# Sparse attention's exponentials cut by halves of the keys, sliding attention's row maximum cut by halves of the heads

## The chip, the core and the metric

The kernel runs on one NeuronCore of a Trainium2 chip. Five engines work from queues of their own, each strictly in the order in which the kernel lists its instructions, and are tied to one another by semaphores only: PE (TensorE, matrix products and transposes), DVE (VectorE), ACT (ScalarE, exponentials and copies), POOL (GpSimd) and SP (SyncE, which starts most DMA transfers). The metric is the device time of one execution in microseconds (us); lower is better.

## The reference

One transformer block for 2048 tokens of width 1024: a projection, three kinds of token mixing side by side, an output projection, a mixture of experts and a gated embedding. The change lies in two of the three mixers.

```python
def dsa_mixer(...):                      # sparse attention, 4 heads
    for each block of 128 queries:       # keys 0 .. end of the block
        sel = top_k(score, 256)
        logits = q @ k[sel] + bias
        probs = softmax(logits)          # exp(l - max) / sum
        out = probs @ v[sel]

def swa_mixer(...):                      # sliding attention, 8 heads, 256 keys a block
    m = maximum(max(logits), sink)
    e = exp(logits - m)
    probs = e / (sum(e) + exp(sink - m))
    out = probs @ v
```

## The kernel before

The selection of the 256 keys has become a mask by the time the function `mixers` starts. `mixers` runs three streams in one: sparse attention (a), sliding attention (w) and the gated linear mixer (g). Each is a list of items; each item has a due time, and all are merged into the one list `items`. Every engine walks through the same list and issues its own part of each item, so the order on each engine is fixed by that list.

**Sparse attention** works in 32 units u: 16 blocks of 128 queries, in the order `ORDER` (block 2, 6, 10, 14, 15, 13, 12, 11, 9, 8, 7, 5, 4, 3, 1, 0), times two pairs of heads. Block j has 128(j+1) keys, that is `steps_of(u)` = j//2+1 steps of 256 keys. The items of a unit:

- Q (u, ci): PE computes the logits of up to 512 keys for two heads into `psL` (L1468; `psL` has one buffer, shared with the item q). DVE adds the mask into `logits` (L1618), takes the maximum of each chunk (L1622, L1633), then of all chunks (L1636) and its negative (L1640).
- E (u, 0) and E (u, 1): ACT takes the exponential in place over all keys of head 0, then of head 1, with the row sum as a by-product into `den` (L1368).
- T (u, sp): PE transposes 256 keys of both heads into a bank of `psX` (L1479), ACT copies the bank to `PT` (L1378). The first T of a unit waits for both exponentials (L1474). `psX` has five banks, used in turn by all three streams.
- V (u, sp): PE multiplies `PT` with the values (L1490), two steps behind its T.
- P and O: ACT copies the result (L1385), PE turns it back (L1499), DVE takes the reciprocal of `den` (L1647) and multiplies (L1652).

For a unit of n steps before it, E (u+1, 0) stands behind step n-3 and E (u+1, 1) behind step n-2 of unit u, so between the two lie one T of unit u with its copy and whatever the other streams have there; with two steps or one, both stand together behind the first step.

**Sliding attention**, block n of 128 queries: q (n, 0) and q (n, 1) each compute half of the eight heads (two of each group of four) into `psL` (L1513); DVE adds the bias into `lg` (L1674). After the second, DVE takes the maximum over all eight heads (L1679), then three small steps (L1680 to L1682); ACT takes eight exponentials (L1390); t, v and o transpose (L1522), multiply (L1535) and turn back (L1543).

When `mixers` ends, SP waits for its last stores, and the next stage (`mix`) starts by loading `o_dram` (L1896).

Of the kernel before, what the change touches and what calls it, by code (L numbers as in the profile page):

```python
# [17 lines left out]
P = 128  # L18
# [992 lines left out]
def mixers(nc, outer, used, kA, small, loads, mask_dram, o_dram, y_dram, ident):  # L1011
# [3 lines left out]
    with ExitStack() as ctx:  # L1015
        def sb(name, shape, dt=F32):
            return ctx.enter_context(nc.sbuf_tensor("p2_" + name, shape, dt))
# [22 lines left out]
        parts = sb("parts", [P, 2, 2, NCH])  # L1040
        den = sb("den", [P, 2, AH])
        rden = sb("rden", [P, 2, AH])
# [40 lines left out]
        biased, top_done, neg_ready, exp_done = sem("biased"), sem("top_done"), sem("neg_ready"), sem("exp_done")  # L1083
        part_done = sem("part_done")
        pv_done, oT_done, rden_done = sem("pv_done"), sem("oT_done"), sem("rden_done")
# [15 lines left out]
        def steps_of(u):  # L1101
            return block_of(u) // 2 + 1


# [243 lines left out]
        def _(act):  # L1348
# [10 lines left out]
            for item in items:  # L1359
                kind = item[0]  # L1360
                if kind == "E":
# [4 lines left out]
                    if (i, h) == (0, 0) and at >= 2:  # L1366
                        act.wait_ge(rden_done, AP2 * (at - 1))
                    act.activation(logits[:, u % 2, h, 0:W], logits[:, u % 2, h, 0:W], ACT.Exp, bias=top[:, u % 4, 1, h:h + 1],  # L1368
                                   accum_out=den[:, at % 2, 2 * i + h:2 * i + h + 1]).then_inc(exp_done, 1)
                    if (i, h) == (1, 0) and at + 1 < NT:  # L1370
# [84 lines left out]
        def _(pe):  # L1455
            pe.wait_ge(both_set, 1)
            for item in items:
# [12 lines left out]
                elif kind == "T":  # L1470
                    u, sp = item[1], item[2]
                    j = block_of(u)
                    if sp == 0:
                        pe.wait_ge(exp_done, 2 * (u + 1))  # L1474
                    until_empty(pe, item)
# [119 lines left out]
        def _(dve):  # L1595
# [9 lines left out]
            for item in items:  # L1605
                kind = item[0]
                if kind == "Q":
# [16 lines left out]
                    else:  # L1624
# [5 lines left out]
                        if u >= 4:  # L1630
                            dve.wait_ge(exp_done, 2 * (u - 3))
                        if ci:
# [8 lines left out]
                elif kind == "O":  # L1641
                    u = item[1]
                    at, i = divmod(u, AP2)
                    dve.wait_ge(exp_done, 2 * (u + 1))
                    if u >= 4:
                        until_read(dve, ("O", u - 4))
                    dve.reciprocal(rden[:, at % 2, 2 * i:2 * i + 2], den[:, at % 2, 2 * i:2 * i + 2]).then_inc(rden_done, 1)  # L1647
                    dve.wait_ge(rden_done, u + 1)
# [6 lines left out]
                elif kind == "q":  # L1655
# [9 lines left out]
                    if n == 0:  # L1665
                        for a in (2 * part, 2 * part + 1):
                            heads = lambda t: t.rearrange("p (g a) k -> p g a k", g=SKV)[:, :, a, first:KEYS]
                            ins = dve.tensor_tensor(heads(lg[:, 0, :, :]), psL[:, :, (a % 2) * KEYS + first:(a % 2 + 1) * KEYS], heads(nearW[:, :, :]), ALU.add)
                            if a % 2 == 0:
                                dve.wait_ge(w_step, after_w(ins))  # L1670
                        ins.then_inc(l_done, 1)
                    else:
                        heads = lambda t: t.rearrange("p (g a) k -> p g a k", g=SKV)[:, :, 2 * part:2 * part + 2, :]
                        dve.tensor_tensor(heads(lg[:, n % 2, :, :]), psL[:, :, :].rearrange("p g (a k) -> p g a k", a=2), heads(nearW[:, :, :]), ALU.add).then_inc(l_done, 1)  # L1674
                    if part == 1:
                        dve.wait_ge(l_done, l_use[item] + 1)
                        if n >= 2:
                            until_read(dve, ("o", n - 2))
                        dve.wait_ge(w_step, after_w(dve.tensor_reduce(st[0], lg[:, n % 2, :, :], AX, ALU.max)))  # L1679
                        dve.wait_ge(w_step, after_w(dve.tensor_tensor(st[1], st[0], sink[:, :], ALU.max)))  # L1680
# [1389 lines left out]
```

## Time and profile before

| | us |
|---|---|
| median of 3 runs | 2882.42 (2882.03 to 2883.32) |
| the profiled execution | 2880.68 |
| its span in the profile | 2879.0 |
| busy in the span | PE 2604.5, DVE 1807.8, ACT 1271.5, POOL 923.4 |

The span is the time from the first to the last instruction in the profile; 1.7 us of the execution lie around it. `mixers` runs from about 845 to 1401 us of the span. Busy time of an engine says how much work it had; what ends a stretch is read from the waits, that is, from what each engine was waiting for when it stood still. The chain that ended last, as the page gives it, covers only the final stage, so it says nothing on this one.

### The profile page before, as it was taken

The page shows a single profiled execution, that of the slowest core. Times are in us where ns is not written, and L with a number is a line of the kernel's source. Part 1 is how long each engine was busy: PE and PEld are TensorE (multiplying, and loading weights), DVE is VectorE, ACT ScalarE, POOL GpSimd, SP SyncE. Part 2 cuts the span into 40 slices and gives each one's busy share as a digit, 9 for nine tenths or more (in the row PEclk, how much of TensorE's full clock was granted, in tenths as well). Part 3 has the DMA queues.
Part 4 walks back from the last instruction along what each step waited for, and adds up shares of the span by engine and source line. Part 5 has one row for each costly group of instructions (what it writes and reads, how often), then busy time and mean ns, then how long its engine had stood idle before and what let it go on. Part 6 is the DMA issues. An engine that isn't in the chain of part 4 may idle for free. (4 is left out here: it accounts for less than half of the span.)

```text
span 2879.0 us, 34808 instructions
## 1 busy us (share of the span) xinstructions
PE 2604.5 (90%) x10908; PEld 1646.4 (57%) x10909; DVE 1807.8 (63%) x2522; ACT 1271.5 (44%) x2289; POOL 923.4 (32%) x925
## 2 busy tenths in 40 slices
PE   6988779999987888878799969999999999998998
PEld 3634323345843444444588846666666676665787
DVE  2176999699976877776333377654464336643676
ACT  2277868958955665665322222222222222221322
POOL 2377877600011111121000024434434335332321
PEclk9999989999989999899799989999999999999999
DMA  5101130113151123212544377986586655974663
GB/s 149 61 31 45 31 61 30 48 56 94 41 183 60 45 68 93 85 53 68 185 147 146 122 292 270 350 321 226 214 333 226 214 203 196 361 275 154 201 218 132
DMA packets 221473, 438.07 MB, mean 152 GB/s; under 512 B 22888, under 2 KB 91048, under 8 KB 221224
## 3 DMA queue, kind: packets, MB, share of 16 engines
q1 hardware_dynamic: 199400, 357.78, 36.3%
q0 software_dynamic: 13312, 47.32, 5.2%
q10 hardware_dynamic: 8640, 31.46, 2.7%
q8 instruction: 62, 1.02, 0.1%
q14 instruction: 59, 0.48, 0.1%
HBM read 331.14 MB, written 105.38 MB: 152 GB/s over the span
## 5 line engine op out<-in xcount | busy, mean ns | idle before, releaser
L2468 DVE CAST p_high<-p_low 128x2048 fp32r<-128x2048 f32 x128 | 203.9, 1593 | 400.1 <-PE p_psG L2575 292.7
L698 PE MATMUL p_psP<-home,p_ring 128*128 128x512 f32 x832 | 366.3, 598 | 0.0
L2591 PE MATMUL p_psY<-p_wd,p_hT 128*128 x752 | 330.9, 593 | 2.2 <-ACT p_hT L2650 1.9
L2470 DVE TENSOR_TENSOR p_low<-p_low,p_high 128x2048 fp32r<-128x2048 f32 x128 | 319.0, 2492 | 4.4
L698 PEld LDWEIGHTS p_psP<-home,p_ring 128*128 128x128 f32 x832 | 157.3, 191 | 205.0 <-issue 204.9
L2591 PEld LDWEIGHTS p_psY<-p_wd,p_hT 128*128 128x128 f32 x752 | 139.3, 190 | 160.5 <-issue 160.4
L727 PE MATMUL p_psI<-p_kI,p_qI 64*128 64x512 f32 (+3 forms) x608 | 148.0, 595 | 62.9 <-ACT p_relu L589 62.8
L2511 POOL TENSOR_TENSOR p_xT_low<-p_xT,p_xT_high 128x512 fp32r<-128x512 f32 x94 | 186.0, 1997 | 3.4 <-ACT p_xT L2635 3.4
L2573 PE MATMUL p_psG<-p_high,p_xT_high 128*128 128x512 f32 x376 | 166.5, 443 | 15.8 <-DVE p_low L2470 8.2
L603 ACT ACTIVATE p_relu<-p_relu,p_small 128x512 f32<-128x512 f32 (+3 forms) x266 | 161.4, 662 | 0.0
L2517 POOL TENSOR_TENSOR p_hid<-p_act_g,p_act_u 128x512 f32<-128x512 f32 x47 | 62.4, 1327 | 308.1 <-ACT p_act_u L2645 295.2
L2573 PE MATMUL p_psU<-p_high,p_xT_high 128*128 128x512 f32 x376 | 154.3, 410 | 6.0 <-DVE p_low L2470 6.0
L2656 ACT ACTIVATE p_y<-p_psY 128x512 f32<-128x512 f32 x94 | 56.2, 598 | 220.3 <-PE p_psY L2591 220.3
L2574 PE MATMUL p_psG<-p_low,p_xT_high 128*128 x376 | 149.7, 398 | 0.0
L2575 PE MATMUL p_psG<-p_high,p_xT_low 128*128 128x512 f32 x376 | 149.7, 398 | 0.0
L589 ACT ACTIVATE p_relu<-p_psI 128x1024 f32<-128x1024 f32 (+3 forms) x152 | 136.4, 914 | 28.6 <-PE p_psI L727 10.4
L2574 PE MATMUL p_psU<-p_low,p_xT_high 128*128 x376 | 148.5, 395 | 0.0
L2575 PE MATMUL p_psU<-p_high,p_xT_low 128*128 128x512 f32 x376 | 148.4, 395 | 0.0
L2641 ACT ACTIVATE p_act_g<-p_psG 128x512 f32<-128x512 f32 x47 | 28.1, 598 | 260.7 <-PE p_psG L2575 260.7
L727 PEld LDWEIGHTS p_psI<-p_kI,p_qI 64*128 64x128 f32 x608 | 50.9, 191 | 152.1 <-ACT p_relu L589 109.9
L2645 ACT ACTIVATE p_act_u<-p_psU 128x512 f32<-128x512 f32 x47 | 28.1, 597 | 240.7 <-PE p_psU L2575 240.7
L1618 DVE SCALAR_TENSOR_TENSOR p_logits<-p_mask,p_psL 128x1024 f32<-128x1024 uint8 (+3 forms) x80 | 84.7, 1059 | 71.5 <-PE p_psL L1468 69.6
(421 smaller groups left out, 5847.4 us busy)
## 6 DMA issues: line engine op xcount, KB each, us to landing
p_low<-in_w_expert_gate_dram SPq DMA_DIRECT2D x32, 2048.0 KB, 13.4
p_low<-in_w_expert_up_dram SPq DMA_DIRECT2D x32, 2048.0 KB, 16.8
p_wd<-in_w_expert_down_dram SPq DMA_DIRECT2D x32, 2048.0 KB, 10.7
y_dram<-p_y ACTq DMA_DIRECT2D x47, 512.0 KB, 8.2
p_xt<-in_x_dram SPq DMA_DIRECT2D x32, 512.0 KB, 4.6
y_dram<-p_clear SPq DMA_DIRECT2D x32, 512.0 KB, 4.5
proj_f<-p_stage SPq DMA_DIRECT2D x52, 256.0 KB, 2.4
p_ot<-o_dram SPq DMA_DIRECT2D x16, 512.0 KB, 4.3
```

What stands on the lines that cost most here:

```text
L589: act.activation(relu[:, n % NRELU, :, 0:c1 - c0], psI[:, n % NI, :, 0:c1 - c0], ACT.Relu).then_inc(relu_done, 1)
L603: act.activation(dst, src, ACT.Copy, scale=small[:, j, h:h + 1]).then_inc(weighed, 1)
L698: mm = pe.matmul(psP[0:n, i % 2, :], w, aT[:, k, c * CH:(c + 1) * CH], start=k == 0, stop=k == KD - 1)
L727: mm = pe.matmul(psI[:, n % NI, half, 0:c1 - c0], qI[r, b % 2, i, :], kI[r, c0:c1], start=True, stop=True)
L1618: dve.scalar_tensor_tensor(out=dst[:, :, c0:c1], in0=hidden, scalar=NEG, in1=psL[:, :, 0:c1 - c0], op0=ALU.mult, op1=ALU.add).then_inc(l_d ...
L2468: dve.tensor_copy(high[:, m, k, :], low[:, par, m, k, :].bitcast(F32)).then_inc(high_done, 1)
L2470: dve.tensor_tensor(low[:, par, m, k, :], low[:, par, m, k, :].bitcast(F32), high[:, m, k, :].bitcast(F32), ALU.subtract).then_inc(w_split, 1)
L2511: pool.tensor_tensor(xT_low[:, k, :], xT[:, k, :], xT_high[:, k, :].bitcast(F32), ALU.subtract).then_inc(xT_split, 1)
L2573: pe.matmul(ps[:, :], xT_high[:, k, :], high[:, m, k, :], start=k == 0, stop=False)
L2574: pe.matmul(ps[:, :], xT_high[:, k, :], left, start=False, stop=False)
L2575: mm = pe.matmul(ps[:, :], xT_low[:, k, :], high[:, m, k, :], start=False, stop=k == KD - 1)
L2591: mm = pe.matmul(psY[:, c, :], hT[:, k, :], wd[:, bass.ds(at, 1), k, c * CH:(c + 1) * CH].rearrange("p a f -> p (a f)"), start=k == 0, sto ...
```

## The change

`halves(u)` cuts the n steps of a unit in two: the first (n+1)//2 steps and the rest; a unit of one step (blocks 0 and 1) stays whole. The item E (u, h) now means "half h of the keys, both heads": two exponentials of half the width where there was one of the full width, each with a sum of its own, for which `den` has another dimension. The first T of a unit waits for the first half only, the T that begins the second half for the second. In item O, DVE adds the two sums into `rden`, waits for that, and takes the reciprocal. In sliding attention, each of q (n, 0) and q (n, 1) takes the maximum of its own four heads, right after adding the bias.

```diff
+        def halves(u):
+            n = steps_of(u)
+            return (0, (n + 1) // 2, n) if n > 1 else (0, n)
+
+        def exps_before(u):
+            return sum(2 * (len(halves(v)) - 1) for v in range(u))
...
-                    act.activation(logits[:, u % 2, h, 0:W], logits[:, u % 2, h, 0:W], ACT.Exp, bias=top[:, u % 4, 1, h:h + 1],
-                                   accum_out=den[:, at % 2, 2 * i + h:2 * i + h + 1]).then_inc(exp_done, 1)
+                    ends = [min(2 * P * sp, W) for sp in halves(u)]
+                    for k, head in [(0, h)] if len(ends) == 2 else [(h, 0), (h, 1)]:
+                        keys = slice(ends[k], ends[k + 1])
+                        act.activation(logits[:, u % 2, head, keys], logits[:, u % 2, head, keys], ACT.Exp, bias=top[:, u % 4, 1, head:head + 1],
+                                       accum_out=den[:, at % 2, k, 2 * i + head:2 * i + head + 1]).then_inc(exp_done, 1)
...
-                    if sp == 0:
-                        pe.wait_ge(exp_done, 2 * (u + 1))
+                    if sp in halves(u):
+                        pe.wait_ge(exp_done, exps_before(u) + 2 * (halves(u).index(sp) + 1))
...
-                    dve.reciprocal(rden[:, at % 2, 2 * i:2 * i + 2], den[:, at % 2, 2 * i:2 * i + 2]).then_inc(rden_done, 1)
+                    mine = slice(2 * i, 2 * i + 2)
+                    if len(halves(u)) == 2:
+                        total = den[:, at % 2, 0, mine]
+                    else:
+                        total = rden[:, at % 2, mine]
+                        dve.tensor_tensor(total, den[:, at % 2, 0, mine], den[:, at % 2, 1, mine], ALU.add).then_inc(summed, 1)
+                        dve.wait_ge(summed, sum(len(halves(v)) == 3 for v in range(u + 1)))
+                    dve.reciprocal(rden[:, at % 2, mine], total).then_inc(rden_done, 1)
...
+                    dve.wait_ge(l_done, l_use[item] + 1)
+                    if part == 0 and n >= 2:
+                        until_read(dve, ("o", n - 2))
+                    mine = lambda t: t.rearrange("p (g a) k -> p g a k", g=SKV)[:, :, 2 * part:2 * part + 2, :]
+                    reduced = after_w(dve.tensor_reduce(st[0].rearrange("p (g a) -> p g a", g=SKV)[:, :, 2 * part:2 * part + 2], mine(lg[:, n % 2, :, :]), AX, ALU.max))
                     if part == 1:
-                        dve.wait_ge(l_done, l_use[item] + 1)
-                        if n >= 2:
-                            until_read(dve, ("o", n - 2))
-                        dve.wait_ge(w_step, after_w(dve.tensor_reduce(st[0], lg[:, n % 2, :, :], AX, ALU.max)))
+                        dve.wait_ge(w_step, reduced)
```

## Rows read from the trace of the kernel before

**Rows 1.** Page, part 1: busy time of each engine over the whole span.
```profile
PE 2604.5 (90%) x10908; PEld 1646.4 (57%) x10909; DVE 1807.8 (63%) x2522; ACT 1271.5 (44%) x2289; POOL 923.4 (32%) x925
```
**Rows 2.** Windows: stretch, length, busy (count) PE PEld DVE ACT POOL, PEclk, DMA share, GB/s.
```profile
845.00:1400.00 555.00, 451.21 (x2556) 242.81 (x2556) 386.07 (x582) 331.83 (x773) 83.00 (x111) 0.91 0.22 70
1176.00:1190.00 14.00, 7.75 (x28) 4.35 (x28) 5.75 (x7) 9.91 (x13) 10.29 (x8) 0.56 0.20 69
```
**Rows 3.** Waits in 845 to 1400: who waited for whom, us, times, longest us.
```profile
PE p_psL L1468 <- DVE p_logits L1618: 28.3, 20, 2.3
PE p_psX L1479 <- ACT p_logits L1368: 24.8, 11, 6.0
PE p_psL L1513 <- DVE p_logits L1618: 11.3, 14, 2.2
PE p_psL L1468 <- DVE p_lg L1674: 8.1, 8, 1.8
...
PE p_psX L1543 <- ACT p_oTW L1407: 5.7, 3, 2.1
...
ACT p_logits L1368 <- DVE p_top L1640: 46.1, 19, 5.5
```
**Rows 4.** Timeline of PE, 855 to 1395: each first T that waited (start, us).
```profile
861.64 1.11 PE L1479 MATMUL p_psX<-ident,p_logits 128*128 128x128 f32 x4 [4.08 <-ACT p_logits L1368]
892.75 0.66 PE L1479 MATMUL p_psX<-ident,p_logits 128*128 128x128 f32 x4 [1.30 <-ACT p_logits L1368]
934.69 0.66 PE L1479 MATMUL p_psX<-ident,p_logits 128*128 128x128 f32 x4 [1.28 <-ACT p_logits L1368]
1038.82 0.66 PE L1479 MATMUL p_psX<-ident,p_logits 128*128 128x128 f32 x4 [2.02 <-ACT p_logits L1368]
1111.39 0.66 PE L1479 MATMUL p_psX<-ident,p_logits 128*128 128x128 f32 x4 [1.22 <-ACT p_logits L1368]
1136.90 0.66 PE L1479 MATMUL p_psX<-ident,p_logits 128*128 128x128 f32 x4 [0.50 <-ACT p_logits L1368]
1181.78 1.11 PE L1479 MATMUL p_psX<-ident,p_logits 128*128 128x128 f32 x4 [6.01 <-ACT p_logits L1368]
1238.71 0.66 PE L1479 MATMUL p_psX<-ident,p_logits 128*128 128x128 f32 x4 [0.75 <-ACT p_logits L1368]
1365.71 1.12 PE L1479 MATMUL p_psX<-ident,p_logits 128*128 128x128 f32 x4 [4.31 <-ACT p_logits L1368]
```
**Rows 5.** Timeline, 1385 to 1432: the first transfer and matmul of the next stage.
```profile
1403.71 0.32 SPq L1896 DMA_DIRECT2D p_ot<-o_dram  x1
...
1407.76 1.97 PE L1948 MATMUL p_psT<-ident,p_ot 128*128 128x128 f32 x8 [7.62 <-DMA p_ot<-o_dram]
```
**Rows 6.** Groups by form, 845 to 1400: count, busy us, mean ns of one, idle before.
```profile
L1390 ACT ACTIVATE p_lg<-p_lg,p_stats 128x256 f32<-128x256 f32 x128 | 63.4, 499 | 8.2 <-DVE p_stats L1682 8.2
L1368 ACT ACTIVATE p_logits<-p_logits,p_top 128x2048 f32<-128x2048 f32 x4 | 8.0, 1992 | 0.0
```
**Rows 7.** Timeline, 1168 to 1190: all engines around the longest wait.
```profile
1173.34 1.58 ACT L1368 ACTIVATE p_logits<-p_logits,p_top 128x1536 f32<-128x1536 f32 x1 [1.95 <-DVE p_top L1640]
...
1178.16 0.59 ACT L1378 ACTIVATE p_PT<-p_psX 128x512 f32<-128x512 f32 x1
...
1180.06 1.57 ACT L1368 ACTIVATE p_logits<-p_logits,p_top 128x1536 f32<-128x1536 f32 x1
...
1184.00 0.58 ACT L1378 ACTIVATE p_PT<-p_psX 128x512 f32<-128x512 f32 x1
...
1185.05 1.22 DVE L1618 SCALAR_TENSOR_TENSOR p_logits<-p_mask,p_psL 128x1024 f32<-128x1024 uint8 x1 [7.10 <-PE p_psL L1468]
```
**Rows 8.** Groups by form of DVE, 845 to 1400: maxima and a small step.
```profile
L1622 DVE TENSOR_REDUCE p_parts<-p_logits 128x2 f32<-128x1024 f32 x42 | 51.3, 1221 | 1.4
L1679 DVE TENSOR_REDUCE p_stats<-p_lg 128x8 f32<-128x2048 f32 x16 | 36.6, 2286 | 0.5
...
L1687 DVE TENSOR_TENSOR p_stats<-p_stats 128x8 f32<-128x8 f32 x16 | 2.5, 156 | 0.0
```

More of the change, by code:

```diff
@@ L1040, in mixers @@
         parts = sb("parts", [P, 2, 2, NCH])
-        den = sb("den", [P, 2, AH])
+        den = sb("den", [P, 2, 2, AH])
         rden = sb("rden", [P, 2, AH])
@@ L1083, in mixers @@
         biased, top_done, neg_ready, exp_done = sem("biased"), sem("top_done"), sem("neg_ready"), sem("exp_done")
-        part_done = sem("part_done")
+        part_done, summed = sem("part_done"), sem("summed")
         pv_done, oT_done, rden_done = sem("pv_done"), sem("oT_done"), sem("rden_done")
@@ L1630, in _ @@
                         if u >= 4:
-                            dve.wait_ge(exp_done, 2 * (u - 3))
+                            dve.wait_ge(exp_done, exps_before(u - 3))
                         if ci:
@@ L1643, in _ @@
                     at, i = divmod(u, AP2)
-                    dve.wait_ge(exp_done, 2 * (u + 1))
+                    dve.wait_ge(exp_done, exps_before(u + 1))
                     if u >= 4:
                         until_read(dve, ("O", u - 4))
-                    dve.reciprocal(rden[:, at % 2, 2 * i:2 * i + 2], den[:, at % 2, 2 * i:2 * i + 2]).then_inc(rden_done, 1)
+                    mine = slice(2 * i, 2 * i + 2)
[6 more added lines that the diff above has]
+                    dve.reciprocal(rden[:, at % 2, mine], total).then_inc(rden_done, 1)
                     dve.wait_ge(rden_done, u + 1)
```

## The prediction, written before the change was run

> **What bounds the kernel now.** I read the page first: PE is busy for 90% of the span, no other engine for more than 63% [rows 1]. The change touches only `mixers`, so the second view is the windows of that stretch, 845 to 1400. PE is busy for 451 of 555 us, DVE for 386, ACT for 332, and the granted clock is 0.91 [rows 2]. PE is the fullest engine here, but about 104 us of it are idle; what the change can win is in these, in the work that runs at half the clock, and nowhere else. The third view is the table of waits. PE's largest are for DVE to free `psL` (28.3, 11.3 and 8.1 us) and, second in the list, 24.8 us in 11 times for the exponentials of L1368 [rows 3]. The fourth is PE's timeline, which gives each of the 11: nine have their row, and the other two, of 1.73 and 1.60 us, are the rest of the 24.8 and belong to block 0, whose units of one step the change leaves whole [rows 3, 4]. What follows the stage isn't loaded ahead: the next stage's first transfer starts at 1403.7 and its first matmul waits for it [rows 5]. So time won in `mixers` moves all that follows, and nothing later hides it.
>
> **Part 1: the first T waits for half of the exponentials.** One exponential takes 499 ns for 256 keys and 1992 ns for 2048 [rows 6], that is (1992-499)/1792 = 0.833 ns a key and 286 ns that don't depend on the width. A pair of halves costs what one full one did, plus 286 ns. So E (u, 0) ends 0.29 us later than now, and the first T may start right behind it instead of behind E (u, 1).
>
> What each wait is worth, by the rows of PE [rows 4]. Seven belong to units whose predecessor has three steps or more, so that a T, its copy and other streams' work stand between the two E: 892.75 (1.30), 934.69 (1.28), 1038.82 (2.02), 1111.39 (1.22), 1136.90 (0.50), 1181.78 (6.01) and 1238.71 (0.75). In each, the first exponential's end plus 0.29 lies ahead of PE's last instruction before the wait, so the whole wait goes: 13.1 us. The two at 861.64 (4.08) and 1365.71 (4.31) have both E side by side right behind the maximum, for 384 and 512 keys; the wait is for the maximum, and only the second pair of short exponentials drops out: 0.5 and 0.7 us (by the formula, two of 384 keys take 2 x 606 ns and two of 256 take 2 x 499, which is 0.2; 512 keys likewise 0.4; a short copy of some 0.3 us that lies between the two E no longer stands ahead of T). Sum 14.3 us.
>
> Does the wait only move? The items behind a T are Q of the next unit and V of a step two back. For the 6.01 us I followed it through [rows 7]. The first E starts at 1173.34 and ends at 1174.9; two copies and a function-table change of another stream come next, then a copy at 1178.16, the second E at 1180.06, another table change and Silu, and a copy at 1184.00. PE could start T at 1175.8 and Q after it, do V when the copy of 1178.16 is there (1179.0 with the 0.29), then q, t and T, and would stand still at the V that needs the copy of 1184.00: with 2 x 0.29 added that is 1185.2. Now PE comes to this V at about 1190.0. So this wait gives 4.8 instead of 6.0, and the rest turns into a wait behind the copy. In the others the copies come with 0.6 us or more in hand. DVE speaks for a real gain: behind this T it stood 7.10 us waiting for Q's matmul [rows 7], so it wasn't the one that held PE. Part 1 gives 14.3 - 1.2 = **-13.1 us**.
>
> **Part 2: ACT pays for it.** 28 units of more than one step take two exponentials more each: 56 x 0.286 = 16.0 us. ACT has 555 - 332 = 223 us idle here [rows 2]; the cover is its waiting for PE and 46.1 us for the maximum [rows 3]. Bounds: at the low end nothing; at the high end all 16.0. What PE waits for of ACT's other work is small, the largest line 5.7 us [rows 3], all such lines together some 19 us by my addition, a fifth to a sixth of PE's idle time. I take that share of 16.0: **+3 us**. Behind each lengthened E on ACT are the copies of T, and PE's V waits for those.
>
> One rule of the Trainium skill speaks against this: "VectorE: DVE Perf Modes", section on the TRN2 errata, says that ScalarE and VectorE pay a fixed latency once per instruction that reads SBUF, and advises tiles of 512 elements or more. The rows agree on the price, 286 ns at any width; blocks below 8 get halves of under 512 keys, and by the rule their 12 units (24 extra exponentials, 6.9 us of ACT) were better left whole.
>
> **Part 3: the sum of the two denominators on DVE.** 28 additions, each a small step with the wait for its result. Nearest row: 156 ns for 128x8 [rows 8]; with the hand-over about 0.2 us: 5.6 us. They stand in item O, ahead of the reciprocal; queued behind are the multiplication into `ostA`, which frees a bank, and the next mask addition, which frees `psL`. Bounds 0 and 5.6.
>
> **Part 4: the sliding maximum in two.** One reduction of 2286 ns becomes two of about 1221 (same element count as L1622) [rows 8]: 0.16 us more each, 16 times, 2.5 us. But it also moves. The one in q (n, 1) is 1.07 us shorter, and DVE had its next work ready in 13 of 16 cases, so 13.9 us come off where DVE is late. The new one in q (n, 0) adds 1.22 us; in 7 of 15 cases DVE stood idle for 0.75 us or more right there, waiting for PE, and hides it, in 8 it delays what is behind: 9.8 us. Net -4.1. Parts 3 and 4 together: 5.6 - 4.1 = +1.5 us of DVE's hurried time. PE's waits for DVE are about half of its idle time [rows 3], but each such microsecond reaches PE only where `psL` or a bank is short; I take a third: **+0.5 us**. Bounds -3 and +8 (all of 5.6 + 2.5). The waits that move with it ask for things that DVE itself did long before and cost nothing. No DMA is moved, and POOL's instructions stay; its waits for earlier work of the linear mixer only shift along.
>
> **Clock.** In 1176 to 1190 the granted clock is 0.56 (nearly all at the lower level, 1.2 GHz), with PE busy for 7.75 of 14 us [rows 2], and the four transposes at 1181.78 take 1.11 us instead of 0.66 [rows 4]. Before this stretch PE had stood still for 6 us. Without it, up to 3.9 us (half of 7.75) would come back, but PE will still stand still for some 4.5 us in the same place. I take nothing, and keep it as a rival.
>
> **Sum.** -13.1 + 3 + 0.5 = -9.6, rounded -9.5 us. The profiled execution took 2880.7, so it would take 2871.2; the median of the runs is 1.7 above it, so the forecast is 2882.4 - 9.5 = **2872.9 us**.
>
> **Rivals.**
> (a) The wait moves. Once PE has run ahead by a T and a Q, it stands at the V behind ACT's copies or at one of the five banks, since ACT is a queue in fixed order and none of its copies comes earlier. For: I found it for the longest wait, 1.2 of 6.0. Against: behind the others the copies are there. If this took two thirds of part 1, -13.1 becomes -4.4, and with the costs -1: 2881.4 us.
> (b) Slower: ACT becomes the bound. The place is the copies queued behind the four exponentials of a unit; the price is 286 ns an exponential, 16.0 us in all, and 8.1 us of DVE's small steps beside it. It decides once more than half of the 24.1 us is on PE's path: at all of it, -13.1 + 24.1 = +11: 2893.4 us. Against it: ACT is idle for 40% of the stage.
> (c) The clock comes back too. Three of the stretches behind a wait ran their T at half speed, 1.11, 1.11 and 1.12 us [rows 4]. If each gives 3 us on top: -9.5 - 9 = -18.5: 2863.9 us. The Trainium skill, "TensorE: Matmul & The Clock Gate", section "Why this matters for your kernels", says that idle gaps between bursts of matmuls throw the clock back, which is this rival; the rows agree for 1181.78, and no row shows that shorter gaps keep it up.
> (d) The change doesn't do what it says for part 1, since a unit's second half is waited for as well. The T that begins the second half comes two to four steps later, behind an E that has long been issued, so I give it nothing but what (a) has.
>
> **How the numbers follow.** Chances: forecast 0.50 (from -6 to -14), (a) 0.27 (from +2 to -6), (c) 0.13 (from -14 to -22), (b) 0.10 (from +2 to +14). A measurement of this kernel can tell some 0.2%, 5.8 us, from no change. Faster by more than that: the forecast's cases, (c), and none of (a): 0.62. Slower by more: half of (b) and a little more, 0.07. Same: the remaining 0.31. The range: down to -20, since (c) reaches there, and up to +3, which holds (a) and the beginning of (b): 2862.4 to 2885.4, with about 0.1 left out on either side in all.
>
> **What would show it.** Right: in the table of waits, PE's 24.8 us for the exponentials fall to about 11 (3.6 + 3.6 + 3.3 for the maxima and block 0 remain), no wait of 6 us is left, ACT's busy time grows by some 16 us plus the read-outs of the sums, DVE's by some 8, and the stage ends 8 to 11 us earlier. If the waits fall and the stage doesn't end earlier, look for PE's waits for `PT` (L1378 before L1490) or for the copies of the other streams: (a). If ACT's idle time for PE is gone, (b). If the granted clock of the stage rises above 0.93, (c). The prediction is wrong altogether if the time changes outside 845 to 1400.

## The result: 0.5% faster, and the profile after

The changed kernel takes 2869.8 us (median of 6 runs, 2864.2 to 2872.0) where the one before takes 2882.2. The ratio is 0.9947, with a 95% interval of 0.9933 to 0.9960, that is 15.3 us less (11.5 to 19.3). The medians alone differ by 12.4. The runs below were made in three later rounds, each with runs of the kernel before beside it, so kernels are compared by their ratios: an effect in us is its ratio less one, times 2882; where two such effects are subtracted, each brings an uncertainty of 2 to 5 us.

The profiled execution took 2864.2 us, the shortest of the six, with a span of 2862.4. Page, part 1, of the kernel after (compare [rows 1]):

```profile
PE 2597.6 (91%) x10908; PEld 1643.8 (57%) x10909; DVE 1810.6 (63%) x2566; ACT 1284.8 (45%) x2401; POOL 923.7 (32%) x925
```

Where the time went is seen at the stage's end: the next stage's first transfer, 1403.71 before [rows 5], is now at 1388.45, and its first matmul waits for it as it did. So 15.3 of the 16.6 us between the spans lie inside `mixers`, and all that follows moved along. Timeline of after (start, us):

```profile
1388.45 0.32 SPq L1916 DMA_DIRECT2D p_ot<-o_dram  x1
...
1392.14 1.97 PE L1968 MATMUL p_psT<-ident,p_ot 128*128 128x128 f32 x8 [7.27 <-DMA p_ot<-o_dram]
```

The windows from the first unit's negative maximum (L1640 before, L1651 after) to that transfer, in both kernels (columns as in [rows 2]); first before, then after:

```profile
849.96:1403.71 553.75, 448.11 (x2543) 241.02 (x2541) 383.58 (x579) 330.97 (x771) 78.62 (x101) 0.91 0.22 69
```
```profile
850.56:1388.45 537.89, 441.42 (x2543) 238.34 (x2541) 386.53 (x623) 344.00 (x883) 79.33 (x101) 0.93 0.23 71
```

PE ran the same 2543 matmuls. Its idle time fell from 105.6 to 96.5 us, which gives 9.2 of the 15.9 us between these windows; the other 6.7 are the same matmuls taking 441.4 instead of 448.1 us, at a granted clock of 0.93 instead of 0.91.

PE's waits in 845 to 1388 of after (compare [rows 3]; L1379 is now the exponential, L1490 the transpose T, L1479 the matmul of Q, L1629 the mask addition, L1692 the sliding bias, L1501 V, L1396 and L1389 ACT's copies):

```profile
PE p_psL L1479 <- DVE p_logits L1629: 27.3, 23, 2.5
PE p_psL L1524 <- DVE p_logits L1629: 10.8, 14, 2.2
PE p_psX L1490 <- ACT p_logits L1379: 10.4, 4, 3.6
PE p_psL L1479 <- DVE p_lg L1692: 8.8, 9, 1.9
PE p_psX L1510 <- ACT p_oT L1396: 8.7, 8, 2.4
PE p_psX L1554 <- ACT p_oTW L1418: 6.6, 3, 2.6
...
PE p_psX L1546 <- ACT p_PTW L1412: 6.0, 4, 2.3
PE p_psX L1490 <- ACT p_PT L1389: 3.4, 3, 2.8
```

The 24.8 us in 11 times for the exponentials became 10.4 in 4, as forecast: what is left are the two units that wait for their maximum and block 0. But the waits for ACT's copies grew. The timeline of after around what was the longest wait [rows 7] shows both:

```profile
1166.93 0.60 PE L1490 MATMUL p_psX<-ident,p_logits 128*128 128x128 f32 x4
...
1167.46 1.13 PE L1479 MATMUL p_psL<-p_kA,near 64*128 64x512 f32 x4
...
1169.77 0.59 ACT L1389 ACTIVATE p_PT<-p_psX 128x512 f32<-128x512 f32 x1
...
1170.41 0.65 PE L1501 MATMUL p_psO<-p_PT,p_small 128*64 128x256 f32 x4 [1.82 <-ACT p_PT L1389]
...
1175.89 0.58 ACT L1389 ACTIVATE p_PT<-p_psX 128x512 f32<-128x512 f32 x1
...
1176.52 0.65 PE L1501 MATMUL p_psO<-p_PT,p_small 128*64 128x256 f32 x4
```

T runs at 1166.9 without a wait, before the second pair of exponentials, Q follows it, V waits 1.82 us for a copy, and the next V stands at 1176.5 right behind its copy of 1175.9, in the order in which the prediction walked it through. The maximum of the next unit comes 13.3 us earlier than before (1184.43 against 1197.74) where that of this unit came 8.7 earlier: 4.6 us, against the forecast 4.8. But the forecast was one of waiting alone. Windows from this unit's maximum to the next one's, before and after:

```profile
1173.14:1197.74 24.60, 18.11 (x92) 9.74 (x92) 15.83 (x21) 18.17 (x28) 10.29 (x8) 0.72 0.21 72
```
```profile
1164.46:1184.43 19.97, 15.81 (x88) 9.08 (x88) 18.23 (x23) 18.41 (x32) 10.32 (x8) 0.85 0.27 88
```

PE's idle time fell by 2.3 us (6.5 to 4.2). The other 2.3 is PE's busy time, at a granted clock of 0.85 instead of 0.72 and with four matmuls fewer between the two marks. (Up to the maximum of unit 18, where both kernels have 259 matmuls, it is 3.0 us of idle time and 2.7 of busy time.) That the two add up to nearly the 4.8 is a coincidence.

What the added work costs its engine, from the groups by form of after (compare [rows 6] and [rows 8]):

```profile
L1697 DVE TENSOR_REDUCE p_stats<-p_lg 128x4 f32<-128x1024 f32 x32 | 39.0, 1220 | 1.1
...
L1663 DVE TENSOR_TENSOR p_rden<-p_den 128x2 f32<-128x2 f32 x28 | 5.3, 191 | 0.0
```

Each of these is as the prediction had it (1221 and some 200 ns), and the exponentials' own time grew from 76.7 to 92.1 us, for a forecast of 16.0 more. ACT is busy for 13.0 us more and DVE for 3.0, where some 8 were forecast: the added reductions and sums are there (2.4 and 5.3 us), but other work of DVE became shorter, above all one pair of updates of `p_state` in the linear mixer. At 1062.24 of the kernel before the pair took 4.32 us while POOL ran two additions of 128x1024, and 1.13 us in the kernel after, where it ran ahead of them. No wait of PE is put down to that pair; DVE stood idle for 1.23 us behind it. Most of this looked like a forecast come true. The experiments say otherwise: the total was right, its parts weren't.

### The profile page after: what moved, and what is told of

It reads as the page before. It is cut to its first block and busy times, and to the rows that moved or that the text cites. A ratio compares the mean times of both kernels' runs of the same rounds, so it can differ in the third digit from the quotient of the medians.

```text
span 2862.4 us, 34991 instructions
## 1 busy us (share of the span) xinstructions
PE 2597.6 (91%) x10908; PEld 1643.8 (57%) x10909; DVE 1810.6 (63%) x2566; ACT 1284.8 (45%) x2401; POOL 923.7 (32%) x925
## 5 line engine op out<-in xcount | busy, mean ns | idle before, releaser
L589 ACT ACTIVATE p_relu<-p_psI 128x1024 f32<-128x1024 f32 (+3 forms) x152 | 136.5, 914 | 28.5 <-PE p_psI L727 10.4
L1479 PE MATMUL p_psL<-p_kA,near 64*128 64x512 f32 (+3 forms) x320 | 84.5, 603 | 42.1 <-DVE p_logits L1629 27.3
```

Source lines behind the costliest of these rows:

```text
L589: act.activation(relu[:, n % NRELU, :, 0:c1 - c0], psI[:, n % NI, :, 0:c1 - c0], ACT.Relu).then_inc(relu_done, 1)
L1479: mm = pe.matmul(psL[:, h, 0:c1 - c0], qA[r, at % 2, i, :], kA[r, c0:c1], start=True, stop=True)
```

## The experiments

### Each half of the change alone

The first kernel puts the sliding maximum back; the second makes only that change.

```diff
# sparse_only, against the changed kernel; sliding_only is the reverse against the kernel before
-                    dve.wait_ge(l_done, l_use[item] + 1)
...
-                    reduced = after_w(dve.tensor_reduce(st[0].rearrange("p (g a) -> p g a", g=SKV)[:, :, 2 * part:2 * part + 2], mine(lg[:, n % 2, :, :]), AX, ALU.max))
                     if part == 1:
-                        dve.wait_ge(w_step, reduced)
+                        dve.wait_ge(l_done, l_use[item] + 1)
...
+                        dve.wait_ge(w_step, after_w(dve.tensor_reduce(st[0], lg[:, n % 2, :, :], AX, ALU.max)))
```

> The changed kernel with the sliding maximum put back to one reduction over all eight heads behind q (n, 1). The result was 12 to 15 us faster than before; the prediction gave -10.1 to the exponentials (-13.1 for the waits, +3 for ScalarE) and about -1 to the sliding maximum (a third of -4.1 plus its own 2.5 already in it). Theory A (the exponentials carry the gain, the clock adds to it): 10 to 14 us faster than before. Theory B (the sliding maximum is worth as much as the exponentials): 5 to 8 us faster.

> The kernel before with only the sliding maximum cut in two. Theory A: 0 to 3 us faster than before, since DVE is relieved by 1.07 us just after q (n, 1) but loaded by 1.22 us after q (n, 0), half of the time under a wait. Theory B: 5 to 8 us faster, the other half of the gain. A slower result, up to 3 us, would mean that the early reduction mostly delays the next mask addition.

Measured: sparse_only 2882.0 us, ratio 0.9992 (0.9983 to 1.0000), 2.3 us faster; sliding_only 2871.7 us, ratio 0.9961 (0.9948 to 0.9974), 11.2 us faster. Theory A fell, and B fell on the other side: the small edit, to which the prediction gave -1.4 us at most, carries most of the gain, and the exponentials alone hardly show. Together they gave 15.3, so on top of the sliding change the exponentials bring about 4 (by ratios with intervals of 4 us on either side, so this 4 isn't shown to differ from nothing), and on top of the exponentials the sliding change brings 13.0.

PE's waits in sparse_only, 845 to 1405, show what became of the exponentials' gain:

```profile
PE p_psL L1479 <- DVE p_logits L1629: 31.7, 21, 3.4
PE p_psX L1490 <- ACT p_logits L1379: 10.6, 4, 3.6
...
PE p_psX L1554 <- ACT p_oTW L1418: 7.0, 3, 2.8
...
PE p_psX L1510 <- ACT p_oT L1396: 6.0, 7, 1.9
PE p_psX L1546 <- ACT p_PTW L1412: 5.9, 4, 2.3
PE p_psO L1501 <- ACT p_PT L1389: 3.2, 3, 1.8
PE p_psX L1490 <- ACT p_PT L1389: 3.0, 2, 2.8
```

and the same lines of the kernel before, 845 to 1400, beside the 5.7 of [rows 3]:

```profile
PE p_psX L1535 <- ACT p_PTW L1401: 4.0, 3, 1.8
PE p_psX L1499 <- ACT p_oT L1385: 3.7, 5, 1.7
...
PE p_psX L1479 <- ACT p_PT L1378: 2.4, 1, 2.4
...
PE p_psO L1490 <- ACT p_PT L1378: 0.2, 1, 0.2
```

The wait for the exponentials is down by 14.2 us here too. But PE's waits for ACT's copies in these lines add up to 25.1 instead of 16.0: 9 us of the 14 came back. That is rival (a); that the copies are late because they stand behind longer exponentials, rival (b)'s reason, is likely and not shown by itself. What was left was lost in another way. Windows of sparse_only over the whole work, then from the maximum of unit 16 to that of unit 18, and the latter in the kernel before:

```profile
849.71:1404.79 555.08, 454.30 (x2543) 245.60 (x2541) 392.59 (x607) 344.90 (x883) 78.58 (x101) 0.90 0.22 69
1191.69:1229.75 38.06, 32.25 (x174) 17.77 (x175) 26.52 (x41) 21.63 (x57) 2.41 (x5) 0.87 0.25 80
```
```profile
1197.74:1231.88 34.14, 27.98 (x167) 15.08 (x165) 26.42 (x41) 19.84 (x48) 2.42 (x5) 0.95 0.29 89
```

PE stood idle for 4.9 us less than before (100.8 against 105.6), but its 2543 matmuls took 6.2 us more. By the start of each unit's negative maximum, sparse_only is 6.0 us ahead of the kernel before at unit 16 (1191.69 against 1197.74), 2.1 at unit 18 and 0.9 behind at unit 29. The 3.9 us between units 16 and 18 are lost in PE's busy time, at a lower clock and with seven matmuls more between the marks, and none in idle time (5.8 us against 6.2).

### What the halves cost when nothing is got for them

```diff
# pay_only, against the changed kernel
-                    if sp in halves(u):
-                        pe.wait_ge(exp_done, exps_before(u) + 2 * (halves(u).index(sp) + 1))
+                    if sp == 0:
+                        pe.wait_ge(exp_done, exps_before(u + 1))
```

> The changed kernel, but the first T of a unit waits for all four exponentials, as before: ScalarE and VectorE pay for the halves (16 us and 5.6 us of instructions) and the waits stay, each 0.57 us longer. The prediction took +3 us for ScalarE and +0.5 for VectorE. Theory A (the price is mostly hidden): 2 to 8 us slower than before, nine waits for the exponentials as before with 24.8 + 9 x 0.6 = some 30 us. Theory B (the price is nearly free): within 2 us of before. Theory C (ScalarE is on the path): over 10 us slower.

Measured: 2891.6 us, ratio 1.0035 (1.0020 to 1.0049), 10.1 us slower than before. This kernel still has the sliding change, worth 11.2, so the price of the halves is some 21 us, and the earlier T gives back some 25 (from 1.0035 to 0.9947). The expectation forgot that the sliding change was in it; with its 11.2 us counted, theory C's number holds; that ScalarE is on the path is another question. Windows of pay_only, then of sliding_only, over the same work:

```profile
847.57:1416.22 568.65, 464.46 (x2543) 248.35 (x2541) 385.90 (x623) 345.88 (x883) 78.63 (x101) 0.88 0.21 67
```
```profile
846.75:1391.16 544.41, 446.54 (x2543) 239.95 (x2541) 379.68 (x595) 330.22 (x771) 78.69 (x101) 0.91 0.22 70
```

Of the 24.2 us between them only 6.3 are idle time of PE (104.2 against 97.9). The other 17.9 are the same 2543 matmuls at a lower granted clock, 0.88 against 0.91. (The profiled execution of sliding_only, 2866.9 us, is the fastest of its six; that of pay_only is at its median.) This is the largest single thing that the prediction left out.

Two more kernels split the price. One adds a short activation per exponential to sliding_only, ScalarE's share without the sums; the other makes the sum in the changed kernel twice.

```diff
# act_extra, against sliding_only, behind each exponential of L1368
+                    if steps_of(u) > 1:
+                        act.activation(spare[:, 0, 2 * u + h:2 * u + h + 1], ident[:, 0:1], ACT.Exp, bias=ident[:, 0:1], accum_out=spare[:, 1, 2 * u + h:2 * u + h + 1])
# sum_twice, against the changed kernel, behind the sum
-                        dve.wait_ge(summed, sum(len(halves(v)) == 3 for v in range(u + 1)))
+                        dve.wait_ge(summed, 2 * sum(len(halves(v)) == 3 for v in range(u + 1)) - 1)
+                        dve.tensor_tensor(total, den[:, at % 2, 0, mine], den[:, at % 2, 1, mine], ALU.add).then_inc(summed, 1)
+                        dve.wait_ge(summed, 2 * sum(len(halves(v)) == 3 for v in range(u + 1)))
```

> The kernel with only the sliding maximum changed (2871.7 us), with one added activation of a single column behind each exponential of L1368 in the units of more than one step: 56 of some 0.29 us, the 16 us that the halves cost ScalarE, without the sums on VectorE and without the earlier T. The kernel that pays for the halves and gets nothing for it took 2891.6, 19.9 us more than 2871.7. Theory ScalarE (most of that is ScalarE's): 10 to 17 us slower than 2871.7. Theory of the prediction (a fifth of 16 us): 2 to 5 us slower. Theory VectorE (the sums, being VectorE work, are dear): under 5 us slower here and the rest in the sums.

> The changed kernel (2869.8 us) with the sum of the two denominators made twice, one behind the other: 28 more small VectorE steps with their waits, some 5.6 us. Theory ScalarE: 0 to 3 us slower than 2869.8. Theory VectorE: 5 to 9 us slower.

> The changed kernel once more, beside the others on the same chip, since the comparison with the seven-unit version rests on a difference of 6 us and six runs of each. Expected at 2869.8, within 2 us.

Measured: act_extra 2879.0 us, ratio 0.9991 (0.9978 to 1.0004), 8.6 us slower than sliding_only; sum_twice 2873.5 us, ratio 0.9965 (0.9953 to 0.9977); the changed kernel again 2867.3 us, ratio 0.9944 (0.9932 to 0.9957). So 28 more sums cost some 6 us by the ratios, give or take 5, or 3.7 against the first median: about as much as they last, and nearer to theory VectorE. How they cost it isn't shown. In the two profiles PE's idle time is the same, 96.7 and 96.5 us, and the whole difference is matmuls at a lower clock (the table below); the profiled execution of sum_twice is the slowest of its six. ScalarE's 16 us cost some 9, between the two theories, 6.2 of it as idle time of PE. The two make 15 of the 21; the rest isn't split (pay_only also lengthens each wait for the exponentials, 27.8 us in 12 times there).

### One wait alone

```diff
# unit15, against the changed kernel without the sliding change
-            return (0, (n + 1) // 2, n) if n > 1 else (0, n)
+            return (0, (n + 1) // 2, n) if n > 1 and u == 15 else (0, n)
```

> The kernel before, with halves for a single unit, number 15 (block 11, second pair), ahead of which TensorE waited 6.0 us; all other units and the sliding maximum as before. The prediction gave 4.8 us to it. Theory A: 4 to 6 us faster, kept to the end of the stage. Theory B (the lead is eaten by later waits for the other streams): under 2 us faster. If the stretch at the lower clock behind this wait (1177 to 1190) also goes, up to 8 us faster.

Measured: 2878.2 us, ratio 0.9980 (0.9971 to 0.9989), 5.8 us faster. With two more exponentials than before, and none of the other 54, the median falls by as much as theory A said. Cutting all 28 units yields 2.3 us, which may be less than cutting this one; the intervals overlap.

The profile doesn't show the lead being kept. Windows of unit15 from its maximum to the next unit's, and from there to that of unit 18 (the kernel before has 24.60 and 34.14 us for the two):

```profile
1173.16:1194.11 20.95, 15.61 (x84) 8.60 (x82) 19.25 (x21) 17.82 (x31) 10.30 (x8) 0.84 0.25 85
1194.11:1232.38 38.27, 32.45 (x176) 17.81 (x176) 26.53 (x41) 20.66 (x49) 2.41 (x5) 0.87 0.26 80
```

It gains 3.6 us and then loses 4.1, which leaves it 0.5 us behind the kernel before at unit 18. Over the two stretches together, with 260 matmuls here and 259 before, PE's idle time is 1.5 us less and its busy time 2.0 more. So the lead didn't come back as a wait: behind the same wait of 2.17 us ahead of a q, PE's work ran at half speed from 1210.8 to about 1221 here, and only from 1212.1 to about 1215 in the kernel before. This execution took 2882.8 us, the second slowest of the twelve (2870 to 2884), so the faster ones must have kept more. The same loss at the same units is in sparse_only above; here it comes without the other 27 units' halves.

### Where VectorE's microsecond stands

The sliding change takes 1.07 us away behind q (n, 1) and adds 1.22 behind q (n, 0). Two kernels separate these. sliding_late makes both reductions of four heads behind q (n, 1); early_extra keeps the old one over eight heads there and adds an unused one behind q (n, 0).

```diff
# sliding_late, against sliding_only
-                    reduced = after_w(dve.tensor_reduce(st[0].rearrange("p (g a) -> p g a", g=SKV)[:, :, 2 * part:2 * part + 2], mine(lg[:, n % 2, :, :]), AX, ALU.max))
                     if part == 1:
+                        for part in range(2):
+                            reduced = after_w(dve.tensor_reduce(st[0].rearrange("p (g a) -> p g a", g=SKV)[:, :, 2 * part:2 * part + 2], mine(lg[:, n % 2, :, :]), AX, ALU.max))
# early_extra, against the kernel before
+                    if part == 0:
...
+                        extra = after_w(dve.tensor_reduce(st[1].rearrange("p (g a) -> p g a", g=SKV)[:, :, 0:2], lg[:, n % 2, :, :].rearrange("p (g a) k -> p g a k", g=SKV)[:, :, 0:2, :], AX, ALU.max))
```

> The kernel before with the sliding maximum in two reductions of four heads each, but both behind q (n, 1), where the one stood. Against the kernel with only the sliding maximum changed (11 us faster than before) it lacks the move. Theory move (the gain is that VectorE is free 1.07 us earlier after q (n, 1)): 0 to 3 us slower than before. Theory chance (any small shift in VectorE's work re-deals the stretches at the lower clock): anything from -8 to +8.

> The kernel before, with the sliding maximum over all eight heads kept behind q (n, 1), and one more reduction over four heads behind q (n, 0) whose result nobody uses: 16 x 1.22 = 19.5 us more work for VectorE, in the place where the change puts its early half. Theory hidden (as the prediction has it, half of these places lie under a wait for TensorE): 2 to 6 us slower than before. Theory free: within 2 us. If VectorE is on the path wherever it has work, 10 us or more slower.

Measured: sliding_late 2887.2 us, ratio 1.0011 (1.0001 to 1.0022), 3.2 us slower than before and 14.4 slower than sliding_only; early_extra 2891.1 us, ratio 1.0030 (1.0017 to 1.0043), 8.6 us slower, above theory hidden and below the last one. So the move is all of it. By these, 19.5 us of work added behind q (n, 0) cost 8.6, 0.44 us each (0.25 to 0.64 by the interval); and taking 17.1 us (16 x 1.07) away behind q (n, 1) is the step from early_extra to sliding_only, -19.8 us, 1.16 us each (some 0.85 to 1.5). Both prices hold the clock: in the profiles, the step of -20.0 us is 11.1 of PE's idle time and 8.9 of faster matmuls.

Two other kernels bear on the higher price. sliding_late has 2.5 us more behind q (n, 1) than the kernel before, for which it would give 2.9 us, and 3.2 were measured, give or take 3. And the pair sparse_only and changed kernel differs by the same move: -13.0 us, beside the -11.2 without the halves. This speaks against theory chance, which would have dealt each kernel a number of its own.

Why the two places differ is seen in one pair. Timeline of the kernel before, DVE's and PE's rows around a q (n, 1), then the same place in sliding_only:

```profile
916.52 2.29 DVE L1679 TENSOR_REDUCE p_stats<-p_lg 128x8 f32<-128x2048 f32 x1
916.64 1.13 PE L1468 MATMUL p_psL<-p_kA,near 64*128 64x512 f32 x4 [0.82 <-DVE p_lg L1674]
...
919.33 1.22 DVE L1618 SCALAR_TENSOR_TENSOR p_logits<-p_mask,p_psL 128x1024 f32<-128x1024 uint8 x1
...
925.61 0.17 DVE L1640 TENSOR_SCALAR p_top<-p_top 128x2 f32<-128x2 f32 x1
```
```profile
912.98 1.22 DVE L1679 TENSOR_REDUCE p_stats<-p_lg 128x4 f32<-128x1024 f32 x1
913.09 1.13 PE L1468 MATMUL p_psL<-p_kA,near 64*128 64x512 f32 x4 [0.82 <-DVE p_lg L1674]
...
914.72 1.22 DVE L1618 SCALAR_TENSOR_TENSOR p_logits<-p_mask,p_psL 128x1024 f32<-128x1024 uint8 x1
...
921.09 0.17 DVE L1640 TENSOR_SCALAR p_top<-p_top 128x2 f32<-128x2 f32 x1
```

Q's matmul was done at 917.8, and the mask addition came only at 919.33, 1.6 us later, behind the reduction and its three small steps; now it comes 0.5 us after the matmul. (PE's matmul of Q itself starts 0.1 us after the reduction in both, since `psL` is free once the bias is added.) From the reduction's start to the negative maximum of the unit, for which ACT's exponentials and then PE's T wait, it is 9.09 us before and 8.11 after. The interval from the reduction to DVE's next other work, over the 16 blocks, has a mean of 3.19 us before and 2.15 in sliding_only. Of the early reductions, 7 of 16 had an idle DVE behind them.

### Is the clock a cause?

```diff
# warm15, against the kernel before
+                    if sp == 0 and u == 15:
+                        for _ in range(16):
+                            pe.matmul(psW[:, 0:P], ident[:, :], ident[:, :], start=False, stop=True, skip_group_check=True)
```

> The kernel before, with 16 added matmuls of the identity with itself, 128 columns each, written to an unused half of a PSUM bank, just ahead of the one T (unit 15) for which TensorE stood still for 6.0 us. They use up some 3 us of that wait and nothing waits for them, so the wait for the exponentials ends when it did. Theory clock (what these changes win is mostly TensorE's granted clock: over six kernels the mean time less half of the time at the lower clock lies between 2763.9 and 2768.4 us, while the times themselves spread over 24 us): the stretch at the lower clock at 1177 to 1190 goes or shrinks, and the kernel gets 2 to 4 us faster although it has more work and keeps the wait. Theory waits (only removed waits count): same as before, within 1 us, or slower by the added work.

Timeline of PE in warm15:

```profile
1175.83 3.74 PE L1476 MATMUL p_psO<-ident 128*128 128x128 f32 x32
1182.01 0.66 PE L1483 MATMUL p_psX<-ident,p_logits 128*128 128x128 f32 x4 [2.44 <-ACT p_logits L1369]
1182.60 2.08 PE L1469 MATMUL p_psL<-p_kA,near 64*128 64x512 f32 x4
...
1187.25 0.66 PE L1526 MATMUL p_psX<-ident,p_lg 128*128 128x128 f32 x4
```

The x32 are the 16 added matmuls, two records each. The T behind the wait took 0.66 us instead of 1.11. The clock fell all the same for the next two rows (2.08 and 1.12 us, half speed) and was full again from 1186.2, where in the kernel before it stayed low until about 1191. The granted clock over 1177 to 1190 was 0.87 instead of 0.53, in part because that stretch now holds added matmuls at full speed; the next unit's maximum came 1.4 us earlier relative to this unit's. So in this place the low stretch follows from PE's standing still, and filling the gap shortened it. But the kernel as a whole took 2882.1 us, ratio 0.9993 (0.9982 to 1.0004), which can't be told from no change, nor from the lower end of the 2 to 4 expected.

How much is clock elsewhere can be read from the same windows of every kernel, from the first negative maximum to the next stage's first transfer, always with 2543 matmuls:

| kernel | median | profiled execution | stage | PE busy | PE idle | clock |
|---|---|---|---|---|---|---|
| before | 2882.2 | 2880.7 | 553.8 | 448.1 | 105.6 | 0.91 |
| changed | 2869.8 | 2864.2 | 537.9 | 441.4 | 96.5 | 0.93 |
| changed, again | 2867.3 | 2868.2 | 539.5 | 443.0 | 96.5 | 0.92 |
| sparse_only | 2882.0 | 2882.4 | 555.1 | 454.3 | 100.8 | 0.90 |
| unit15 | 2878.2 | 2882.8 | 554.9 | 449.5 | 105.5 | 0.91 |
| sliding_only | 2871.7 | 2866.9 | 544.4 | 446.5 | 97.9 | 0.91 |
| sliding_late | 2887.2 | 2886.9 | 561.3 | 453.0 | 108.3 | 0.90 |
| early_extra | 2891.1 | 2888.9 | 564.4 | 455.4 | 109.0 | 0.89 |
| act_extra | 2879.0 | 2877.6 | 552.7 | 448.6 | 104.1 | 0.91 |
| pay_only | 2891.6 | 2891.6 | 568.6 | 464.5 | 104.2 | 0.88 |
| sum_twice | 2873.5 | 2879.4 | 554.8 | 458.2 | 96.7 | 0.89 |
| picked (next section) | 2863.7 | 2860.6 | 536.7 | 443.0 | 93.8 | 0.92 |
| picked_short (next section) | 2859.5 | 2860.8 | 532.6 | 441.5 | 91.1 | 0.92 |

Idle time and clock move together in most steps, but not in all: sum_twice has the idle time of the changed kernel and 15 us more of matmuls. Over all runs, not only the profiled ones, the mean span times its granted clock (the span as if the clock had been full throughout, which also counts idle time at the low clock) is 2762.2 us for sliding_only and 2764.1 for pay_only, whose mean times lie 21 us apart; the kernel before has 2766.7 and the changed one 2763.7. So here much of the difference between kernels goes along with the clock. What sets it, the waits as in warm15 or something else besides, stays open, and so does the share of the 6.7 us that the change itself caused.

### A version that beats both

picked cuts only the seven units in front of which PE waited for the second exponential. picked_short also makes two small steps of the three behind the sliding maximum.

The diff leaves out that `neg_sink` is made once and that ScalarE counts `w_neg` in twos.

```diff
# picked, against the changed kernel
-            return (0, (n + 1) // 2, n) if n > 1 else (0, n)
+            return (0, (n + 1) // 2, n) if n > 1 and u in (3, 5, 9, 12, 13, 15, 18) else (0, n)
...
# picked_short, against picked
-                        dve.wait_ge(w_step, after_w(dve.tensor_tensor(st[1], st[0], sink[:, :], ALU.max)))
-                        dve.wait_ge(w_step, after_w(dve.tensor_tensor(st[3], sink[:, :], st[1], ALU.subtract)))
-                        dve.tensor_scalar(st[2], st[1], -1.0, None, ALU.mult).then_inc(w_neg, 1)
+                        dve.scalar_tensor_tensor(out=st[2], in0=st[0], scalar=-1.0, in1=neg_sink[:, :], op0=ALU.mult, op1=ALU.min).then_inc(w_neg, 1)
+                        dve.wait_ge(w_neg, 2 * n + 1)
+                        dve.tensor_tensor(st[3], sink[:, :], st[2], ALU.add).then_inc(w_neg, 1)
```

> The changed kernel with halves for seven units only (3, 5, 9, 12, 13, 15, 18), those in front of which TensorE waited for the second exponential in the kernel before. ScalarE pays 14 extra exponentials instead of 56 (4.0 us instead of 16.0), VectorE 7 sums instead of 28. Theory price (ScalarE's extra work is what ate the gain of the exponentials): 3 to 8 us faster than the changed kernel, 2862 to 2867. Theory clock alone: within 3 us of the changed kernel.

> The kernel with halves for seven units (2863.7 us), with the chain behind the sliding maximum cut from three small VectorE steps to two: the negative of the maximum with the sink comes in one step and is signalled at once, the difference to the sink follows it. 16 x 0.2 = 3.2 us less VectorE work in the place behind q (n, 1), and ScalarE's exponentials can start 0.4 us earlier. By the measured worth of a microsecond in that place (19.4 us gained for 17.1 us taken away): 3 to 4 us faster, 2860. If the last steps lie under a wait: within 1 us of 2863.7.

Measured: picked 2863.7 us, ratio 0.9937 (0.9920 to 0.9953). Against the changed kernel that is 2 to 6 us better, by which of the two measurements and by ratio or median one goes; the intervals overlap, so it is likely and not shown. picked_short 2859.5 us, ratio 0.9912 (0.9899 to 0.9925), 25 us faster than before and clear of the changed kernel's 0.9944 (0.9932 to 0.9957), measured beside it. The step from picked is -7 us, give or take 6, where 3 to 4 were expected; both agree with the higher price. Windows of picked_short:

```profile
850.73:1383.30 532.57, 441.52 (x2543) 238.30 (x2541) 378.30 (x587) 332.78 (x799) 79.18 (x101) 0.92 0.23 72
```

DVE is busy for 8 us less than in the changed kernel, ACT for 11 less, and PE idles for 91.1 us instead of 96.5.

## Why the prediction was right, and where it was wrong

The forecast was 2872.9 us, 9.5 less than before, within 2862.4 to 2885.4; 2869.8 lies in it, on the faster side. The medians' 12.4 us less lie in the forecast's own case (6 to 14 less), the ratio's 15.3 at the near end of rival (c)'s (14 to 22 less). The stage ended 15.3 us earlier, not 8 to 11. That the sum came out near enough is luck: the gain of the halves, their price and the gain of the sliding maximum were all put far too low, and the errors had opposite signs. The halves with their price brought 2 to 4 us where the sum gave them some 8, the sliding maximum 11 to 13 where it gave 1.4.

- **Part 1, the waits (-13.1).** The waits went as foreseen: seven gone, only maxima and block 0 left. But as idle time it brought less than forecast, 7.7 us from pay_only to the changed kernel (104.2 to 96.5), and for the longest wait 2.3 instead of 4.8. The ratios give it some 25 us in all; the rest came with the clock, 0.88 to 0.93 in the windows.
- **Part 2, ScalarE (+3).** The instructions were right (286 ns each), the share on PE's path was not: I took a fifth, from the size of PE's visible waits for ACT's other lines (and my 19 us for these left out one wait of 6.0). About half of it (8.6 of 16 us, give or take 5) came through. The waits seen in the profile of before say how often ACT is late now, not how near it is to being late; 9 us of new waits appeared in lines that had had 16.
- **Part 3, the sums (a third of 5.6).** By the times all of it, some 6 us; the profiles don't show it as idle time of PE.
- **Part 4, the sliding maximum (-4.1 of VectorE's time, a third of it PE's).** This is the step that failed most plainly, by a factor of eight: -1.4 us in the sum, -11.2 measured. The direction was right and so were the instructions' times, but I multiplied the difference of two amounts (13.9 and 9.8 us) by a third. Measured on the full amounts, 17.1 and 19.5 us, a microsecond behind q (n, 1) is worth 1.16 us and one behind q (n, 0) 0.44; the difference of two numbers with different weights isn't weighted by a mean of them. (The weights are worked out from the -11.2 and the 8.6, so they can't confirm them; sliding_late and picked_short are what they were tried on.)
- **Clock (0).** I kept it out of the sum and gave rival (c) 0.13. It was part of the result: 6.7 us of the stage's 15.9, at 0.93, the very value above which rival (c) was to be believed. Where a wait is removed or added it belongs in the price, both ways: against sliding_only it made up 17.9 of pay_only's 24.2 us.
- **Rivals.** (a) happened to the exponentials: 9 of 14 us moved to ACT's copies. (b)'s price was paid in full in pay_only (some 21 us for the halves' 16.0 and 5.6), though more of it as clock than as waiting. (c) came in part. (d) didn't happen: the four waits for exponentials that are left (861.7, 1350.1, 1371.6 and 1375.5) all stand at first T.
- On the rule of the Trainium skill ("VectorE: DVE Perf Modes", the TRN2 errata, tiles of 512 elements or more): from unit 20 to the last, blocks 7 and below, sparse_only lost 4.2 us against the kernel before and the changed kernel gained nothing, while picked, which leaves these units whole, gained 3.5, so in these profiles it pointed the right way. Width and wait aren't told apart by this, since none of the seven waits stood in front of these units. My count by the rule was off as well: block 7 gets halves of 512 keys, and the second half of block 8 has 384 keys.

## What to carry to other kernels

Weigh each microsecond by the place in which it stands, and weigh what is taken and what is added separately: on an engine 70% busy, a microsecond of the same kind of reduction cost 0.44 us in one place and 1.16 in another, and in the pair shown the dearer place is the one where the next work of that engine lay ready. Cut work in two only where something waits for the first half; elsewhere the fixed price is paid for nothing. When an edit's parts can be run alone, do it before believing a total that fits. And when a profile's number fits a forecast, split it into idle and busy time first.

## What the runs showed of the hardware beyond that

The same 2543 matmuls took between 441.4 us (clock 0.93) and 464.5 us (clock 0.88) in two kernels that differ only in what PE waits for. Behind the same wait of 2.17 us, PE's work at half speed lasted some 3 us in the profile of the kernel before and some 10 in that of unit15. And the runs of one kernel scatter: the 12 of unit15 over 2870 to 2884 us, those of the kernel before over 2880 to 2891, 2878 to 2892 and 2877 to 2890 in three rounds, so a difference of 3 us needs many runs here.
